# Hybrid mLSTM/pooling block: branch and output projections written out per quarter, with the pooling branch first

## The chip, the cores and the metric

One core of one Trainium2 chip. The metric is the time of one execution in microseconds, as the device measures it, of the whole kernel with the inputs in HBM. The kernel is in 32-bit floats throughout.

## The reference, cut to what matters

The layer projects 2048 latent tokens (and 256 context tokens) of width 1024 into q, k, v, gates and the inputs of a pooling branch, scans them with a two-way mLSTM, and then does this, which is all that the change touches:

```
hn  = h * rsqrt(mean(h*h per head) + eps) * head_norm_w      # h: sum of both scan directions
y_m = (hn * sigmoid(o) * silu(z_m)) @ branch_m_w             # 1024 x 1024
mixed = (box means of p - p) per group @ pool_w[group]       # 4 groups of 128
y_p = (mixed * pool_scale * silu(z_p)) @ branch_p_w          # 512 x 1024
m   = sigmoid(g_m) * y_m + sigmoid(g_p) * y_p
x   = x + gate * (m @ out_w)                                 # 1024 x 1024
out = rmsnorm(x, final_norm_w)
```

## The kernel before

Every engine's program is written out by hand, and semaphores order them. Four earlier stages (norm, two input projections, the scan with the rest of the input projection beside it) are not changed, but for two weight tiles named below. The fifth stage computes the lines above, from 2001 us to the end. It reads what the earlier stages stored in HBM: `hsum_d` (h), `u_d` (the gate of the hidden branch), `mix_d`, `zp_d` (pooling branch), `gm_d`, `gp_d` (merge gates).

The stage takes the tokens in four **quarters** of 512. Features lie on the 128 partitions. A **unit** is one block of 128 output features of one product: 8 units "m" (hidden branch, 8 feature blocks deep), 8 units "p" (pooling branch, 4 deep) and 8 units "o" (output projection, 8 deep), 24 in a quarter. Each product of 32-bit numbers is made of three matmuls of high and low parts (L1779: `wh*bh`, `wh*bl`, `wl*bh`), so that a unit m or o is 24 matmuls of 128x512, and a unit p is 12.

- Weights: SyncE loads a tile into `wraw` (2 buffers, L1625), ScalarE copies its high part to `wh` (L1823), VectorE makes the low part `wl` (L1934; 3 buffers each). A p tile is 128x512, the others are 128x1024.
- Before the units of a quarter the **hidden** inputs are made: square sums on ScalarE (L1831), norms on VectorE (L1947), 8 transposes on TensorE (`turn_hidden`, L1730), gating into `yt` (VectorE, L1958), high part `y_h` (ScalarE, L1845), low part `y_l` (GpSimd, L2064). The **pooled** inputs of a group: `mix_h` (ScalarE, L1850), `mix_l` (GpSimd, L2069), three matmuls (`group`, L1741), `ypt` (VectorE, L1968), `yp_h` (L1855), `yp_l` (GpSimd, L2073).
- `merge`: units m and p alternate. For each feature block VectorE gates both results out of PSUM (`merged_m` L2003, `merged_p` L2013), adds them (L2016), and ScalarE and VectorE split the sum into `m_h`, `m_l`.
- `out_proj`: units o. ScalarE scales a result (`of`, L1861), TensorE turns it back (`turn_output`, L1787), VectorE adds it to `xo` (L1977). In between stands the work for the next quarter: the tables NORM, GATE, SPLIT, GROUP say beside which unit.
- The final norm (`out_square` L1867, `out_stats`, `out_norm` L1988) and the store follow in the next quarter's merge.

The first quarter's preparation and merge are written out, then a hardware loop of three rounds runs `out_proj` of a quarter and `merge` of the next (`quarters`); the last `out_proj` is written out. Every queue is in order, also SyncE's, where a load that waits holds up all behind it.

Of the kernel before, what the change touches and what calls it, by code (L numbers as in the profile page):

```python
# [11 lines left out]
P = 128  # L12
D = 1024
# [11 lines left out]
PG = 4  # L25
# [21 lines left out]
def hybrid_block(nc, x, c, ctx, c_ctx, norm_w, ada_w, ada_b, in_w, gate_b, head_norm_w, pool_w,  # L47
# [29 lines left out]
    with ExitStack() as top:  # L77
# [793 lines left out]
        with ExitStack() as ph:  # L871
# [9 lines left out]
            W_BEFORE = 2 + HEADS * NU  # L881

# [84 lines left out]
            load_at = [0 if p == 1 else split_at[2 * p - 1] + 1 if p else None for p in range(NT // 2)]  # L967

# [250 lines left out]
            def _(act):  # L1219
# [60 lines left out]
                for t in range(NSLOT):  # L1280
# [7 lines left out]
                    for p in range(1, NT // 2):  # L1288
                        if load_at[p] == t:
                            pair(p)  # L1290
                    if 0 <= l + 1 < NHALF:
                        copy_scores(l + 1)
                    for m in ending(t):
                        evacuate(m)
                    for u in range(2, NT):
                        if split_at[u] == t:
                            split_hi(u)
                    if 0 <= l + 1 < NL:
                        weights_hi(l + 1)
# [7 lines left out]
            def _(dve):  # L1307
# [95 lines left out]
                for t in range(NSLOT):  # L1403
# [19 lines left out]
                    for u in range(2, NT):  # L1423
                        if split_at[u] == t:
                            split_lo(u)
                    if 0 <= l + 1 < NL:
                        weights_lo(l + 1)
# [104 lines left out]
        weights.close()  # L1532

        with ExitStack() as ph:
# [4 lines left out]
            WS = 3  # L1542
            wraw = sb("wraw5", [P, 2, KT, P])
            wh = sb("wh5", [P, WS, KT, P], FP32R)
            wl = sb("wl5", [P, WS, KT, P], FP32R)
# [20 lines left out]
            mp_ = sb("merged_p", [P, TQ])  # L1566
# [7 lines left out]
            oss = sb("oss", [P, 4, QT])  # L1574

            w_loaded = [sem(f"w5_loaded{n}") for n in range(2)]
            w_hi = sem("w5_hi"); w_lo = sem("w5_lo"); unit_done = sem("unit_done")
            rows_loaded = sem("rows_loaded"); rows_ready = sem("rows_ready")
# [8 lines left out]
            g_loaded = [sem(f"g5_loaded{n}") for n in range(2)]  # L1587
            gated = sem("gated"); m_made = sem("m_made"); m_hi = sem("m_hi"); m_lo = sem("m_lo")
            of_made = sem("of_made"); o_turned = sem("o_turned"); x_loaded = sem("x5_loaded")
            x_added = sem("x_added"); o_act = sem("o_act"); o_dve = sem("o_dve"); o_ready = sem("o_ready")  # L1590
            o_stored = sem("o_stored")


            UNITS = [(m, n, kt) for n in range(KT) for m, kt in (("m", KT), ("p", PG))] + [("o", n, KT) for n in range(KT)]
            NU = len(UNITS)
# [4 lines left out]


            NORM = {1: 0, 2: 1, 3: 2, 4: 3}
# [5 lines left out]
            def quarters(eng, out_proj, merge, last):  # L1608


                with eng.Fori(0, NTQ - 1) as i:
                    out_proj(i, True)
                    merge(i + 1, True)
                out_proj(NTQ - 1, False)
                last(NTQ - 1)

            @block.sync
            def _(sp):
                sp.sem_inc(o_stored, 1)

                def tile(i, u):
                    m, n, kt = UNITS[u % NU]
                    sp.wait_ge(w_hi, i * NU + (u + 1))
                    sp.wait_ge(w_lo, i * NU + (u + 1))
                    sp.dma_start(wraw[:, u % 2, 0:kt], SRC[m][:, :, n * P:(n + 1) * P]).then_inc(w_loaded[u % 2], 16)  # L1625

                def hidden(i, q):

                    if not isinstance(i, int):
                        sp.wait_ge(h_turned, i * QT + (q + 1 - QT))  # L1630
                    sp.dma_start(hsum[:, q], hsum_d[i * QT + q]).then_inc(h_loaded[q], 16)

                def hidden_gate(i, q):

                    sp.wait_ge(y_made, i * QT + (q + 1))
                    sp.dma_start(ut[:, q % 2], u_d[:, :, bass.ds(i * TQ + q * P, P)].rearrange("j p t -> p j t"))\
                        .then_inc(u_loaded[q % 2], 16)

                def pooled(i, g):
                    sp.wait_ge(yp_made, i * PG + (g + 1))  # L1640
                    sp.dma_start(mixt[:, g % 2], mix_d[g, :, bass.ds(i * TQ, TQ)]).then_inc(mix_loaded[g % 2], 16)
                    sp.dma_start(zpt[:, g % 2], zp_d[g, :, bass.ds(i * TQ, TQ)]).then_inc(mix_loaded[g % 2], 16)

                def gates(i, n):
                    sp.wait_ge(gated, i * (2 * KT) + (2 * n + 1))
                    sp.dma_start(gmt[:, n % 2], gm_d[n, :, bass.ds(i * TQ, TQ)]).then_inc(g_loaded[n % 2], 16)
                    sp.dma_start(gpt[:, n % 2], gp_d[n, :, bass.ds(i * TQ, TQ)]).then_inc(g_loaded[n % 2], 16)

                def store(i, q):
                    sp.wait_ge(o_ready, i * QT + (q + 1))  # L1650
                    sp.dma_start(out[bass.ds(i * TQ + q * P, P), :], xo[:, q, :]).then_inc(o_stored, 16)

                def residual_x(i, q):
                    sp.dma_start(xo[:, q, :], x[bass.ds(i * TQ + q * P, P), :]).then_inc(x_loaded, 16)

                def merge(i, after):
                    for n in range(KT):
                        tile(i, 2 * n + 3)
                        tile(i, 2 * n + 4)
                        if n + 2 < KT:  # L1660
                            gates(i, n + 2)
                        if n > KT - QT:
# [452 lines left out]
```

## Time and profile before

| | us |
|---|---|
| median of 3 runs (lowest, highest) | 2601.05 (2599.51, 2602.22) |
| the profiled execution's own time | 2600.4 |
| its span, first to last instruction | 2598.4 |
| TensorE busy (share of the span) | 2421.3 (93%) |
| VectorE, ScalarE, GpSimd busy | 1208.2, 785.4, 314.1 |
| granted TensorE clock, mean | 0.969 of full |

The span is 2.0 us below the time of the same execution, and that time is 0.65 us below the median. A share of busy time is a mean over stages; the fifth stage is the last 597 us of the span. "Issue" in the rows is idle time for which the profile shows no releaser.

### The profile page before, as it was taken

How to read it: one execution, taken by the hardware profiler on the slowest of the kernel's cores; microseconds unless marked ns; L12 is line 12 of the kernel's file. 1: busy time of each engine (PE TensorE's matmuls, PEld its weight loads, DVE VectorE, ACT ScalarE, POOL GpSimd, SP SyncE). 2: the span in 40 equal slices, each digit the busy share in tenths (PEclk: the TensorE clock that was granted, in tenths of full speed). 3: DMA queues.
4: the chain of work that ended last, by engine and by line, in shares of the span. 5: the costliest groups of instructions: out<-in, count | busy, mean ns of one | idle time of the engine just before them, and what ended most of it. 6: DMA issues, size and time to landing. Idle time of an engine off the chain costs nothing. (4 is left out here: it accounts for less than half of the span.)

```text
span 2598.4 us, 35271 instructions
## 1 busy us (share of the span) xinstructions
PE 2421.3 (93%) x12267; PEld 2018.6 (78%) x12267; DVE 1208.2 (46%) x2352; ACT 785.4 (30%) x1609; POOL 314.1 (12%) x323
## 2 busy tenths in 40 slices
PE   6897999999999998999999989999998598989897
PEld 4766888888888877888888877888887487777776
DVE  2612212212222224566666646777674555555553
ACT  2521111111111112343333323434432433343432
POOL 0011000000000001121112111321120202030300
PEclk8998999999999999999999999999999699999998
DMA  7457544534434457877787889876775574646653
GB/s 228 129 63 225 134 98 117 131 98 117 131 97 117 123 117 186 227 224 225 221 248 209 212 259 216 245 231 199 214 219 174 173 228 127 212 150 191 184 177 106
DMA packets 472916, 453.42 MB, mean 175 GB/s; under 512 B 24268, under 2 KB 414052, under 8 KB 471228
## 3 DMA queue, kind: packets, MB, share of 16 engines
q1 hardware_dynamic: 433132, 387.74, 51.2%
q10 hardware_dynamic: 32240, 32.51, 8.0%
q0 software_dynamic: 7392, 31.15, 3.1%
q8 instruction: 95, 1.56, 0.2%
q14 instruction: 57, 0.47, 0.1%
HBM read 311.25 MB, written 140.05 MB: 174 GB/s over the span
## 5 line engine op out<-in xcount | busy, mean ns | idle before, releaser
L1190 PE MATMUL bank<-xlate,wh 128*128 128x512 f32 x2048 | 673.1, 402 | 12.8 <-DVE v_t L1310 4.9
L1190 PEld LDWEIGHTS bank<-xlate,wh 128*128 128x128 f32 x2048 | 374.7, 190 | 84.1 <-DMA xlate<-xe_d 6.1
L1190 PE MATMUL bank<-xlate,wl 128*128 128x512 f32 x1024 | 411.0, 401 | 0.0
L625 PE MATMUL bank<-xearly,wh 128*128 128x512 f32 (+1 forms) x1280 | 368.5, 373 | 0.2 <-issue 0.2
L625 PE MATMUL bank<-xlate,wh 128*128 128x512 f32 x1024 | 321.3, 395 | 0.0
L625 PEld LDWEIGHTS bank<-xearly,wh 128*128 128x128 f32 x1280 | 229.3, 189 | 40.2 <-issue 0.7
L625 PE MATMUL bank<-xearly,wl 128*128 128x512 f32 (+1 forms) x640 | 237.4, 371 | 0.0
L625 PEld LDWEIGHTS bank<-xlate,wh 128*128 128x128 f32 x1024 | 190.7, 189 | 39.3
L1190 PEld LDWEIGHTS bank<-xlate,wl 128*128 128x128 f32 x1024 | 194.3, 190 | 34.4
L625 PE MATMUL bank<-xlate,wl 128*128 128x512 f32 x512 | 201.2, 393 | 0.0
L831 DVE SCALAR_TENSOR_TENSOR qks<-bank,qks 128x512 fp32r<-128x512 f32 (+1 forms) x72 | 47.5, 661 | 304.1 <-ACT qks L701 304.1
L1934 DVE TENSOR_TENSOR wl<-wraw,wh 128x1024 fp32r<-128x1024 f32 x96 | 110.8, 1154 | 122.6 <-ACT wh L1823 122.5
L1333 DVE SCALAR_TENSOR_TENSOR state<-state,cols,bank 128x516 f32<-128x516 f32 x128 | 95.7, 748 | 120.3 <-PE bank L1151 120.3
L625 PEld LDWEIGHTS bank<-xearly,wl 128*128 128x128 f32 x640 | 120.6, 188 | 21.2
L1823 ACT ACTIVATE wh<-wraw 128x1024 fp32r<-128x1024 f32 x96 | 87.3, 909 | 148.9 <-DMA wraw<-in_branch_p_w_dram 84.5
L1164 PE MATMUL bank<-state_h,q_t 128*128 128x258 f32 x512 | 114.7, 286 | 10.1 <-DVE den L1389 10.1
L1151 PE MATMUL bank<-v_t,ek_h 128*128 128x258 f32 x576 | 112.0, 286 | 7.4 <-DVE ek_l L1315 7.4
L625 PEld LDWEIGHTS bank<-xlate,wl 128*128 128x128 f32 x512 | 96.4, 188 | 21.9
L1779 PE MATMUL bank<-m_h,wh 128*128 128x512 f32 x256 | 105.8, 413 | 6.2 <-DVE wl L1934 5.6
L1304 ACT ACTIVATE ysb<-bank 128x258 f32<-128x258 f32 x128 | 49.5, 386 | 198.2 <-PE bank L1151 197.7
L1779 PE MATMUL bank<-y_h,wh 128*128 128x512 f32 x256 | 101.3, 396 | 8.2 <-POOL y_l L2064 6.6
L1338 DVE TENSOR_TENSOR wl<-wraw,wh 128x1024 fp32r<-128x1024 f32 x62 | 79.2, 1278 | 59.0 <-ACT wh L1238 59.0
(226 smaller groups left out, 4103.5 us busy)
## 6 DMA issues: line engine op xcount, KB each, us to landing
v_t<-vk_d SPq DMA_DIRECT2D x144, 384.0 KB, 4.3
qk_d<-qks SPq DMA_DIRECT2D x64, 512.0 KB, 2.7
q_t<-qk_d SPq DMA_DIRECT2D x128, 256.0 KB, 5.5
wraw<-in_in_w_dram ACTq DMA_DIRECT2D x31, 1024.0 KB, 11.9
wraw<-in_in_w_dram SPq DMA_DIRECT2D x32, 512.0 KB, 9.0
vk_d<-vs SPq DMA_DIRECT2D x64, 256.0 KB, 2.7
k_t<-qk_d SPq DMA_DIRECT2D x64, 256.0 KB, 6.6
wraw<-in_branch_m_w_dram SPq DMA_DIRECT2D x32, 512.0 KB, 4.0
```

Of the source, the lines that this page charges most:

```text
L625: mm = pe.matmul(bank[m % 4][:, 0:w], a[:, u % 2, k, :], xn(b, k, t0, w), start=(k == 0 and n == 0), stop=(k == KT - 1 and n == 2))
L831: dve.scalar_tensor_tensor(out=qks[:, a % 2, 0:cw, 1, :], in0=bank[m % 4][:, 0:w].rearrange("p (c t) -> p c t", t=P), scalar=HD ** -0.5 if ...
L1151: mm = pe.matmul(ubank[:, b, 0:VW], e_[:, L, b * P:(b + 1) * P], v_t[:, V, va, :], start=(n == 0), stop=(n == 2))
L1164: pe.matmul(XBANK[:, 0:VW], q_t[:, l % QS, b, qa, :], c_[:, L, b, :], start=(b == 0 and n == 0), stop=(b == HB - 1 and n == 2))
L1190: mm = pe.matmul(bank[m % 2][:, :], a[:, u % 2, k, :], xlate[part][:, k, tq * TQ:(tq + 1) * TQ], start=(k == 0 and n == 0), stop=(k == KT ...
L1304: act.activation(ysb[:, :], YBANK[:, 0:VW], ACT.Copy).then_inc(y_read, 1)
L1333: dve.scalar_tensor_tensor(out=state[:, ch], in0=state[:, ch], scalar=col(d, NC + latent_chunk(l), 4, h), in1=upair[:, :, 0:VW], op0=ALU.m ...
L1338: dve.tensor_tensor(wl[:, u % 2], wpair[:, :, u % 2 * P:(u % 2 + 1) * P], f32(wh[:, u % 2]), ALU.subtract).then_inc(w_lo, 1)
L1779: mm = pe.matmul(dst[:, :], a[:, u % WS, k, :], b[:, k, :], start=(k == 0 and r == 0), stop=(k == kt - 1 and r == 2))
L1823: act.activation(wh[:, u % WS, 0:kt], wraw[:, u % 2, 0:kt], ACT.Copy).then_inc(w_hi, 1)
L1934: dve.tensor_tensor(wl[:, u % WS, 0:kt], wraw[:, u % 2, 0:kt], f32(wh[:, u % WS, 0:kt]), ALU.subtract).then_inc(w_lo, 1)
```

## The change

The loop is gone: all four quarters are written out, and a quarter has three phases. Pooled phase: the 8 units p. The gated results are held in `mp_`, which now lies over the buffer `hsum` (freed as its tokens are turned). Hidden phase: the 8 units m, each result merged with the held one. Output phase: the 8 units o.

- Weights of the pooling branch come as 4 tiles 128x1024, each for two units, so that a quarter has 20 tiles and not 24. The buffers are those of the scan's stage; the first two tiles are loaded and split there, in its last slots.
- SyncE loads tile T+4 in step T, after tile T+2 has been split. The other loads of a step stand behind it.
- First quarter: all four groups come first, and `pw` is waited for alone (before: together with `hw_row`). Its hidden inputs are normed and turned after units p1, p3, p5, p7.
- Later quarters: groups before units o1, o2, o4, o5, each split a step earlier; token tile 0 turned before o5, tile 1 before o7, tiles 2 and 3 after the units p3 and p5 of the new quarter.
- The final norm's squares are taken in two parts: 896 columns once 7 of 8 blocks are added, then 128; the statistics are one instruction longer. In the last quarter the first part stands ahead of the last `output`.

```diff
+            def gate_pooled(i, n):                       # VectorE, into the held results
+                dve.wait_ge(unit_done, i * NU + n + 1)
+                dve.wait_ge(gp_loaded[n % 2], 16 * ((i * KT + n) // 2 + 1))
+                if n % 2 == 0:
+                    dve.wait_ge(h_turned, i * QT + n // 2 + 1)
-            NORM = {1: 0, 2: 1, 3: 2, 4: 3}
-            GATE = {3: 0, 4: 1, 5: 2, 6: 3}
-            SPLIT = {1: 0, 3: 1, 4: 2, 6: 3}
-            GROUP = {2: 0, 4: 1, 5: 2, 7: 3}
+            SPLIT = {0: 0, 1: 1, 3: 2, 4: 3}
+            GROUP = {1: 0, 2: 1, 4: 2, 5: 3}
+            NORM = {1: 0, 2: 1, 3: 2, 4: 3}
+            TURN_O = {5: 0, 7: 1}
+            TURN_P = {1: 2, 2: 3}
+            # pooled unit n, TensorE
+                if n < 2: pe.wait_ge(yp_made, (i + 1) * PG - 1 + n)
+                else:     pe.wait_ge(p_gated, i * KT + n - 1)
+            # ScalarE, pooled phase of a later quarter
+                if i and t == 0: output(i - 1, KT - 1)
+                split_hi(T + 2)
+                if t == 0:
+                    hidden_hi(i, 1)
+                    for q in range(QT): out_square(i - 1, 0, q)
+                if t == 1:
+                    for q in range(QT): out_square(i - 1, 1, q)
+                if t == 2: out_root(i - 1)
+                if t in TURN_P: hidden_hi(i, TURN_P[t])
+            # SyncE, output phase, step n
+                tile(T + 4)
+                if n < QT: hidden(i + 1, n)
+                if n in (2, 3): pooled(i + 1, n)
```

GpSimd during one output phase of a loop round. First before (`mix_l` is what a group waits for, `y_l` the low part of 128 turned tokens):

```order
L2064 TENSOR_TENSOR y_l<-yt,y_h 128x8x128
L2068 REGISTER_ALU
L2069 TENSOR_TENSOR mix_l<-mixt,mix_h 128x512
L2064 TENSOR_TENSOR y_l<-yt,y_h 128x8x128
L2068 REGISTER_ALU
L2069 TENSOR_TENSOR mix_l<-mixt,mix_h 128x512
L2073 TENSOR_TENSOR yp_l<-ypt,yp_h 128x512
L2064 TENSOR_TENSOR y_l<-yt,y_h 128x8x128
```

Now the same work of one quarter:

```order
L2153 TENSOR_TENSOR mix_l<-mixt,mix_h 128x512 x2
L2157 TENSOR_TENSOR yp_l<-ypt,yp_h 128x512 x2
L2153 TENSOR_TENSOR mix_l<-mixt,mix_h 128x512 x2
L2157 TENSOR_TENSOR yp_l<-ypt,yp_h 128x512 x2
L2148 TENSOR_TENSOR y_l<-yt,y_h 128x8x128 x4
```

No `mix_l` stands behind a `y_l` of its quarter any more.

VectorE at the turn from an output phase to the pooled phase. Before, from the last round's second merge step (`merged_p` is the gating of a unit p):

```order
L1934 TENSOR_TENSOR wl<-wraw,wh 128x1024
L2003 SCALAR_TENSOR_TENSOR merged_m<-gmt,bank 128x512
L1933 REGISTER_ALU
L1934 TENSOR_TENSOR wl<-wraw,wh 128x512
L2013 SCALAR_TENSOR_TENSOR merged_p<-gpt,bank 128x512
```

Now, in the last quarter (`hsum<-gpt,bank` is the same gating, into the held results; `yt` is the gating of turned tokens):

```order
L1996 TENSOR_TENSOR wl_c<-wraw,wh_c 128x1024
L2065 TENSOR_TENSOR xo<-bank,xo 128x4x128
L2018 TENSOR_TENSOR yt<-bank,ut 128x512 x2
L2038 SCALAR_TENSOR_TENSOR hsum<-gpt,bank 128x512 x2
L1996 TENSOR_TENSOR wl<-wraw,wh 128x1024
L2038 SCALAR_TENSOR_TENSOR hsum<-gpt,bank 128x512 x2
L2018 TENSOR_TENSOR yt<-bank,ut 128x512 x2
L1996 TENSOR_TENSOR wl<-wraw,wh 128x1024
L2071 TENSOR_TENSOR oss<-oss 128x4
L2073 TENSOR_SCALAR oss<-oss 128x4
L2075 RECIPROCAL oss<-oss 128x4
L2038 SCALAR_TENSOR_TENSOR hsum<-gpt,bank 128x512 x2
```

The gating of units p2, p4 and p6 now stands behind a weight split, and that behind ScalarE's work.

ScalarE at the end of the program (`of` is `output`, `junk_o` a square sum). Before:

```order
L1861 ACTIVATE of<-bank,mgate 128x512 x4
L1867 ACTIVATE junk_o,oss<-xo 128x1024 x4
L1871 ACTIVATE oss<-oss 128x4
```

Now:

```order
L1916 ACTIVATE of<-bank,mgate 128x512 x3
L1926 ACTIVATE junk_o,oss<-xo 128x896 x4
L1916 ACTIVATE of<-bank,mgate 128x512
L1926 ACTIVATE junk_o,oss<-xo 128x128 x4
L1931 ACTIVATE oss<-oss 128x4
```

Four square sums moved ahead of the last `output`.

## Rows read from the trace of the kernel before

**Rows 1.** Stretches of the fifth stage: start:end, length, busy of each engine, clock, DMA.
```profile
2001.50:2054.40 52.90, 12.96 (x44) 9.09 (x45) 29.57 (x47) 22.07 (x54) 19.46 (x12) 0.57 0.65 199
2054.40:2059.90 5.50, 5.50 (x13) 4.33 (x14) 0.83 (x1) 0.00 (x0) 0.00 (x0) 0.50 0.32 95
2054.40:2582.90 528.50, 490.89 (x2176) 401.60 (x2176) 275.29 (x379) 184.58 (x328) 62.81 (x36) 0.97 0.56 170
2582.90:2598.40 15.50, 0.66 (x4) 0.42 (x4) 6.59 (x8) 5.04 (x10) 0.00 (x0) 0.59 0.34 135
```

**Rows 2.** TensorE's waits, 2054 to 2583: us in total, times, longest.
```profile
PE bank L1741 <- issue: 24.7, 11, 3.7
PE bank L1779 <- DVE wl L1934: 12.3, 7, 2.6
PE bank L1779 <- POOL y_l L2064: 6.6, 1, 6.6
```

**Rows 3.** TensorE in order of time: start, length; without and after a long pause.
```profile
2114.30 0.39 PE L1779 MATMUL bank<-y_h,wh 128*128 128x512 f32 x1
...
2115.21 0.39 PE L1779 MATMUL bank<-y_l,wh 128*128 128x512 f32 x1
...
2152.46 0.63 PE L1779 MATMUL bank<-m_l,wh 128*128 128x512 f32 x1
2152.89 0.63 PE L1779 MATMUL bank<-m_h,wl 128*128 128x512 f32 x1
```

**Rows 4.** TensorE, pauses (us idle before, in brackets).
```profile
2151.38 0.47 PE L1741 MATMUL bank<-mix_h,pw_h 128*128 128x512 f32 x1 [3.16 <-issue]
...
2246.29 0.49 PE L1779 MATMUL bank<-y_h,wh 128*128 128x512 f32 x1 [1.59 <-DVE wl L1934]
...
2253.83 0.49 PE L1779 MATMUL bank<-yp_h,wh 128*128 128x512 f32 x1 [1.79 <-DVE wl L1934]
```

**Rows 5.** GpSimd in order of time, before the pause that ends at 2151.38.
```profile
2147.71 2.35 POOL L2064 TENSOR_TENSOR y_l<-yt,y_h 128x1024 fp32r<-128x1024 f32 x1 [7.13 <-ACT y_h L1845]
2150.02 1.26 POOL L2069 TENSOR_TENSOR mix_l<-mixt,mix_h 128x512 fp32r<-128x512 f32 x1
```

**Rows 6.** Groups, 2054 to 2583: busy us, mean ns of one, idle before.
```profile
L1934 DVE TENSOR_TENSOR wl<-wraw,wh 128x1024 fp32r<-128x1024 f32 x63 | 80.8, 1283 | 69.9 <-ACT wh L1823 69.9
L1823 ACT ACTIVATE wh<-wraw 128x1024 fp32r<-128x1024 f32 x62 | 65.0, 1049 | 34.4 <-PE bank L1779 18.9 <-DMA wraw<-in_out_w_dram 15.3
L2064 POOL TENSOR_TENSOR y_l<-yt,y_h 128x1024 fp32r<-128x1024 f32 x13 | 30.8, 2370 | 63.8 <-ACT y_h L1845 63.8
...
L2013 DVE SCALAR_TENSOR_TENSOR merged_p<-gpt,bank 128x512 f32<-128x512 f32 x32 | 21.9, 683 | 15.4 <-PE bank L1779 15.4
...
L1958 DVE TENSOR_TENSOR yt<-bank,ut 128x512 f32<-128x512 f32 x24 | 15.3, 676 | 0.0
```

**Rows 7.** Loads, 2060 to 2583: count, KB each, median us from issue to landing.
```profile
hsum<-hsum_d SPq DMA_DIRECT2D x12, 512.0 KB, 7.6
...
mixt<-mix_d SPq DMA_DIRECT2D x12, 256.0 KB, 5.5
```

**Rows 8.** The 32 loads of `gpt`, 256 KB each.
```profile
DMA to landing us min/median/max: 3.6/4.0/6.9
```

**Rows 9.** ScalarE's first instruction of the fifth stage.
```profile
2014.61 0.63 ACT L1910 ACTIVATE pw_h<-pw 128x512 fp32r<-128x512 f32 x1 [12.72 <-DMA hw_row<-in_head_norm_w_dram]
```

**Rows 10.** VectorE: two of a tile's four norms, beside GpSimd and without it.
```profile
2022.29 1.90 DVE L1947 SCALAR_TENSOR_TENSOR hsum<-hsum,hss,hw_row 128x256 f32<-128x256 f32 x2
...
2134.41 0.88 DVE L1947 SCALAR_TENSOR_TENSOR hsum<-hsum,hss,hw_row 128x256 f32<-128x256 f32 x2
```

**Rows 11.** The end of the chain that ended last: start, us, what.
```profile
2582.45 0.69 ACT of L1861
2583.15 0.05 issue
2583.19 0.67 PE bank L1787 x4
...
2584.61 1.16 ACT junk_o L1867 x2
...
2585.85 1.16 ACT junk_o L1867 x2
```

More of the change, by code:

```diff
@@ L1653, in residual_x @@
[L1653 to L1662, printed above, removed]
-                            q = n - (KT - QT + 1)
-                            if after:
-                                sp.wait_ge(o_stored, (i - 1) * (16 * QT) + (16 * (q + 1) + 1))
-                            residual_x(i, q)
-                        if after and n >= KT - QT:
-                            store(i - 1, n - (KT - QT))
@@ new lines, in hidden_unit, with ready @@
+                def hidden_unit(i, n):
+                    weights_ready(i * NT5 + M0 + n)
+                    if n >= 2:
+                        pe.wait_ge(m_gated, i * KT + n - 1)
+                    elif i:
+                        pe.wait_ge(of_made, (i - 1) * KT + KT - 1 + n)
+                    def ready(k):
+                        if n == 0 and k == 0:
+                            pe.wait_ge(y_hi, (i + 1) * QT)
+                            pe.wait_ge(y_lo, (i + 1) * QT)
+                    products(bank[n % 2], weight(i * NT5 + M0 + n), (y_h, y_l), 0, KT, ready)
@@ L1788, in turn_output @@
                     mm.then_inc(o_turned, 1)
-                def merge(i, after):
-                    for u in range(2 * KT):
-                        unit(i, u)
-                        if after and u == 0:
+                pe.wait_ge(pw_lo, 1)
+                for g in range(PG):
+                    group(0, g)
+                for i in range(NTQ):
+                    for n in range(KT):
+                        pooled_unit(i, n)
+                        if i and n == 0:
                             turn_output(i - 1, KT - 1)
-                def out_proj(i, ahead):
+                        if i == 0 and n % 2 == 1:
+                            turn_hidden(0, n // 2)
+                        elif i and n % 2 == 1 and n // 2 in TURN_P:
+                            turn_hidden(i, TURN_P[n // 2])
@@ L1980, in out_stats @@
                 def out_stats(i):
[L1981 to L1985 removed]
+                    a = i * (2 * QT + 1)
+                    dve.wait_ge(o_act, a + 2 * QT)
@@ L2047, in _ @@
-                for q in range(QT + 1):
-                    if q < QT:
-                        norms(0, q)
-                    if q > 0:
-                        branch(0, q - 1)
-                        gate_hidden(0, q - 1)
-                    if q in (1, 2):
-                        split_lo(0, q - 1)
-                dve.wait_ge(rows_loaded, 48)
-                merge(0, False)
-                quarters(dve, out_proj, merge, last)
+                branch(0, 0)
+                branch(0, 1)
@@ L2059, in _ @@
+                i = NTQ - 1
+                residual(i, KT - 2)
+                residual(i, KT - 1)
+                out_stats(i)
+                for q in range(QT):
+                    out_norm(i, q)
             @block.gpsimd
```

673 lines of the change are left out of this document (377 added, 296 removed).

## The prediction

> **What bounds the kernel now.** I read the waits of TensorE first, then cut the last stage into stretches. From 2054.4 to 2582.9, 528.5 us, TensorE is busy for 490.9 us [rows 1], and its waits there are 24.7 us ahead of groups and 12.3 us on the weights' low part (plus 0.6 us in a wait not shown) [rows 2]: 37.6 us in all, the whole idle time. VectorE is busy for 275 us of the stretch, so no helper engine is full; what waits is order. Ahead of the stretch lie 52.9 us with 13.0 us of TensorE, behind it 15.5 us with 0.7 us [rows 1]. So the fifth stage takes 596.9 us, and for 92 us of that TensorE idles (39.9, 37.6 and 14.8).
>
> A pause has a second price. Matmuls of 128x512 start every 0.227 us at the full clock (0.91 us for four) and every 0.43 us after a long pause [rows 3]: the two levels of 2.4 and 1.2 GHz. After the 3.16 us pause 10 matmuls run slowly, 1.7 us more; after 1.79 us too, after 1.59 us not [rows 4]. In order of time I count nine such runs of 7 to 10 matmuls behind nine pauses of 1.79 us or more, together 14.7 us, and one of 12 at 2054.4 (2.4 us; the clock is 0.50 of full for 5.5 us [rows 1]). The full-clock work of the stretch is therefore 528.5 - 37.6 - 17.1 = 473.8 us.
>
> **The head, 2001.5 to 2054.4.** Three things move. First, ScalarE begins only when `hw_row` has landed, at 2014.6, for the sake of `pw` [rows 9]; `pw` is a fifth of the 1.3 MB issued until then and now goes first, so I put the first group at 2014 instead of 2020.9. Second, the four groups run without hidden tiles between them; but `ypt` has one buffer, and each later group waits for the split of the one before and for a load that waits for a gating. With 5.5 us for a `mixt` load [rows 7] I follow them to 2028.5, when unit p0 begins; its last quarter waits to 2033 because ScalarE takes tile 0's square sums and root ahead of the last `yp_h`. Third, the pooled units then run between the norms. Per pair of units (5.5 us at the full clock) VectorE has a weight split of 1.28, two gatings of 0.68, two of 0.68 for `yt` [rows 6], and four norms: two of them take 1.90 us beside GpSimd and 0.88 without it [rows 10], so up to 3.8, with half a microsecond for the root. That is 8.3 at the worst and 6.2 at the best; I take 7.3 from the walk, since about half of the norms lie beside a `y_l` of 2.37 us. Four pairs from 2033 less the part of p0 already done give 2061; then the last tile needs its weight split, gatings, `y_h` (1.05, as a split of that size) and `y_l` (2.4): the hidden phase begins at 2067. The second weight tile of the branch adds a split of 1.28 us to VectorE's last slot of the scan: 1.1 us more. Head: 66.9 us instead of 52.9, but with 8 pooled units in it, 8 x 12 x 0.227 = 21.8 us. Net gain 7.8. Bounds: 60 us (loads land at once, norms without GpSimd) to 76 us (loads as long as `hsum`'s 7.6 [rows 7]).
>
> The Trainium skill (SBUF — State Buffer, "Who interferes with whom") says that a VectorE operation with two SBUF inputs and a GpSimd operation exclude each other for a whole instruction. The stretched norms agree with it. By that rule each norm or split that meets a `y_l` of 2.37 us could wait for all of it; over four pairs the head would then be about 4 us longer than by the rows.
>
> **The output phases (three with a next quarter).** Now a group waits mostly because GpSimd makes a `y_l` of 2.35 us and only then `mix_l` [rows 5]. The pauses are about 3.2 to 3.7 us twice a quarter, 0.3 to 1.3 otherwise, 24.7 us in all [rows 2]. With the new order no `mix_l` is behind a `y_l`, and the turned tiles were normed steps earlier, so these waits go. What is late next are the loads: SyncE's step n now begins after the split that follows the end of unit o(n-1), about 2.5 us into unit o(n), where a split done one unit earlier released it. `mixt` for group 2 is issued at about 17.0 us of the phase, lands 5.5 to 6 later, takes 0.6 on ScalarE (as the 128x512 copy of [rows 9]) and 1.3 on GpSimd [rows 5], and is ready at 25.1 when TensorE wants it at 24.5; group 3 likewise 1 us late. Sum 1.7 us; if `hsum` takes its full 7.6 us [rows 7], ScalarE is later too and the phase loses 5.5, with one such half-clock stretch. I take 2.5 per phase, nearer the short case, as the loads of a step are now 1 to 1.5 MB and were 2 MB. 3 x 2.5 = 7.5 us; bounds 0 and 17.
>
> **The pooled phases (three behind an output phase).** The weight waits of 12.3 us [rows 2] came from p tiles loaded in short steps; a tile now serves 5.5 us of units and is loaded four tiles ahead, 22 us against a split of 1.05 + 1.28 and a load: no wait. But gating is behind other work. ScalarE in step 0 does `output`, a split, `y_h`, and four square sums at a pitch of 1.24 us for 1024 columns [rows 11], about 1.13 for 896. `y_h` waits for VectorE's `yt` until 5.5; the squares end at 11.1; the next split at 12.2 and its low part at 13.4; only then is unit p2 gated, at 14.1, and TensorE wanted that bank for p4 at 12.5. Pause 1.65 us. The same way p6 waits 0.85 us (the statistics are in front), and the hidden phase begins on `y_l` with no pause to speak of. Sum 2.6 us. The first pause lies between the 1.59 that kept the clock and the 1.79 that lost it [rows 4], so half of a half-clock stretch, 0.8 us, is added: 3.4 per phase, 3 x 3.4 = 10.2 us. Bounds 1 and 24, the latter being the second rival.
>
> **The hidden phases** hold 5.44 us of matmuls per unit against 3.4 us of VectorE (a split of 1.28 and three steps of 128x512 at 0.68 or 0.69 [rows 6]), 1.7 of ScalarE (1.05 and 0.63): no loss. The output phase's first unit asks for the last `m_l` 2.9 us after the last unit m, and uses it at 4.8: none. The written-out code costs nothing that I can see: the first merge is written out already and runs at 0.227 [rows 3]. The Trainium skill (Runtime: NRT & Kernel Launch, "Instruction fetch mechanics") says that a taken branch out of the fetched window stalls; no pause at a loop's edge is left unexplained here, so I count no gain.
>
> **The tail.** The last `of` (0.69) starts at once after the last unit, then turning 0.67, addition 0.7, four square sums at 1.24 [rows 11]. Now ScalarE's queue has the four sums of 896 columns ahead of the last `of`, and they wait for block 6, 1.3 us after the unit. They end at 5.8; `of`, turning and addition end at 8.0. A copy of 512 columns takes 0.63 [rows 9] and of 1024 takes 1.05 [rows 6], 0.82 ns a column, so a sum of 128 columns has a pitch of 1.24 - 0.73 = 0.5 (and one of 896 of 1.13); four end at 10.0, against 7.1 before. With the extra instruction (0.2): +3.1 us. Bounds 0 and 4.
>
> **Sum.** Before: 52.9 + 528.5 + 15.5 = 596.9. After: head 66.9; then 473.8 - 21.8 = 452.0 of work, 2.4 of slow clock after the 6 us pause at the head's end, 7.5 and 10.2: 472.1; tail 18.6. Together 557.6, which is 39.3 less. The profiled execution took 2600.4 us, so 2561.1; the median of the runs is 0.65 above it: 2562.
>
> **The rivals.**
> 1. *The queues are as good as they look in the first merge*: no pause in the output phases and only the short one in the pooled phases, as the losses I add (17.7 us) come from a walk with uncertain landings. For it: 22 us of lead for weights, lighter traffic. Against: the square sums' place is certain. 4 us of loss instead of 17.7 and 2 off the head: 2546.
> 2. *The merge gates' loads pace the pooled phases.* `gpt` has two buffers; a load starts after a gating, and two units later its data is needed. Before, two units meant 16 us, now 5.5. For it: landing took up to 6.9 us [rows 8], and a 512 KB weight tile is now issued ahead of it. Then a pair takes 6.9 + 0.7 + 0.1 = 7.7 instead of 5.5: 6.7 us in three pairs, in four quarters 27, less the 10.2 that it replaces: 2579; with 1.7 at half clock behind half of the twelve pauses up to 2589. Against: the median is 4.0 us, and 4.8 fits under 5.5.
> 3. *Slower: the late loads of the output phase hold up ScalarE's in-order queue.* Square sums wait for `hsum`, then the split, `of` and `mix_h` behind them, so each of the four groups and the turns wait as two do now. Price: a pause of 3.7 and 1.7 for the clock at each of four groups, 21 us a phase, 63 in three, less the 7.5 that it replaces: 2618. It decides from 16 us a phase up (39.3 / 3 + 2.5), that is with landings of 10 us or more after issue. The longest median is 7.6 [rows 7], and there is less traffic per step; so it is unlikely.
> 4. *The change doesn't shorten anything*: the four quarters are still bound by the same chain, the pauses only change places, 2601. The rows speak against it, as the pauses have named causes that the order removes.
>
> **How the numbers follow.** My forecast, 2549 to 2574: 0.60. Rival 1, below 2549: 0.15. Rival 2, 2574 to 2595: 0.19. Rival 4: 0.02. Rival 3: 0.04. The head's bounds are -7 and +9, the phases' -17 and +24, the tail's -3 and +1; not all fall on one side, so the range of 8 in 10 is 2543 to 2583. A measurement of this kernel tells about 0.2% (5.2 us) from no change. Faster by more: 0.94; within: 0.02; slower: 0.04.
>
> **What would show it.** In the new profile: the groups' 24.7 us of waits fall below 6; the weights' 12.3 us to nearly 0; the first group starts near 2014 and the hidden phase near 2067; a pause of 1 to 2 us ahead of unit p4 in three quarters, released by the gating; after the last unit four square sums before `of`, and a tail of 18.6 us. The prediction is wrong if pauses ahead of pooled units repeat at every pair with `gpt` as the releaser of the gating (rival 2), if groups wait for `mix_l` behind a load (rival 3), or if the first quarter's pooled units take over 9 us a pair.

## The result and the profile after

| | before | after |
|---|---|---|
| median of four runs, us | 2600.28 (2597.1 to 2602.22) | 2510.23 (2509.72 to 2513.99) |
| ratio | | 0.9658 [0.9641, 0.9675] |
| profiled execution; its span | 2600.4; 2598.4 | 2509.72; 2507.9 |
| scan begins / ends, us of the span | 970.3 / 2001.5 | 946.6 / 1957.7 |
| fifth stage, scan's end to the span's | 596.9 | 550.2 |

The forecast was 2562 us in a range of 2543 to 2583. The change gained 90 us, not 39, and the time lies below the range. (In later sets of runs the kernel before took 2592 to 2597 us; against that the gain is 82 to 87 us.) The spans of the two profiled executions differ by 90.5 us, and these fall into two parts: 46.7 us in the fifth stage (forecast 39.3), and 43.8 us in front of it (forecast 0), where the code differs only in two weight tiles that are loaded and split in the scan's last slots.

The stretches of the fifth stage after, which answer to [rows 1] (head, first to last unit, tail; start:end, length, busy us of TensorE, its weight loads, VectorE, ScalarE and GpSimd with their instructions, clock, DMA share, GB/s):

```profile
1957.70:2026.20 68.50, 34.21 (x141) 25.39 (x140) 38.78 (x58) 24.34 (x56) 19.68 (x12) 0.77 0.63 200
2026.20:2489.10 462.90, 452.47 (x2080) 372.19 (x2080) 260.75 (x353) 180.23 (x331) 61.14 (x36) 1.00 0.59 185
2489.10:2507.90 18.80, 1.12 (x4) 0.72 (x4) 6.77 (x9) 6.56 (x18) 0.00 (x0) 0.61 0.28 112
```

TensorE's waits after, from 2026 us on, which answer to [rows 2] (us in total, times, longest):

```profile
PE bank L1782 <- DVE hsum L2038: 7.1, 6, 1.3
PE bank L1782 <- POOL y_l L2148: 6.3, 1, 6.3
PE bank L1840 <- ACT of L1916: 5.8, 1, 5.8
PE bank L1774 <- issue: 2.8, 3, 1.5
```

The groups' 24.7 us are 2.8, the weights' 12.3 us are none, and the pooled units of the later quarters wait six times for a gating (`hsum` is here the tile that holds the gated products). The 6.3 us end the head, the 5.8 us are the tail's.

The earlier stages: TensorE's longest waits before its last stage, first of before, then of after.

```profile
PE bank L216 <- DMA aw<-in_ada_w_dram: 12.9, 5, 3.2
PE bank L596 <- ACT ymaj L698: 11.0, 1, 11.0
PE bank L1164 <- DVE den L1389: 10.1, 4, 3.9
PE bank L1151 <- DVE ek_l L1315: 7.4, 4, 2.3
```
```profile
PE bank L216 <- DMA aw<-in_ada_w_dram: 10.2, 8, 3.5
...
PE bank L596 <- ACT ymaj L698: 5.4, 1, 5.4
PE bank L1172 <- DVE den L1407: 5.2, 4, 1.8
...
PE bank L1159 <- DVE ek_l L1333: 0.6, 1, 0.6
```

The same waits stand in both, shorter after. ScalarE's instructions are the same in both kernels up to the scan, so they tell where the 43.8 us lie: 5.0 us by its 41st instruction (76.4 us before, 71.4 after), 18.3 between the 81st and the 161st (112.8 to 384.4 before, 107.9 to 361.2 after), 0.5 from there to the scan's begin, and 20.0 in the scan. The first 5 us are chance: the other kernels whose scan ends late reach that instruction at 70.7 to 72.8 us, those whose scan ends early at 70.9 to 75.3.

The DMA queues differ too. For 117 to 900 us (queue; packets, MB, share of 16 engines' time), before and after:

```profile
q1 hardware_dynamic: 99941, 84.88, 45.7%
```
```profile
q1 hardware_dynamic: 103843, 87.12, 37.4%
```

For 4% more packets the transfer engines are busy for a fifth less: 16 x 783 us x 0.457 / 99,941 is 57 ns for a packet before, and 45 ns after. A 512 KB weight tile of the input projection landed after 9.0 us before and 7.7 after. In the scan itself queue q1 takes 50 ns for a packet in both, and it is the queue of ScalarE's loads, q10, that differs; its row for the scan, before and after:

```profile
q10 hardware_dynamic: 32240, 32.51, 20.2%
```
```profile
q10 hardware_dynamic: 33296, 33.56, 12.7%
```

That is 103 ns and 62 ns for a packet. A packet's time is not the time that a stage loses, though: the 1024 KB tiles of this queue land after 11.9 us before and 12.6 after, and from ScalarE's 161st to its 281st instruction (384 to 845 us before) both kernels take the same 460 to 461 us, with slow packets and with fast ones.

### The profile page after: what moved, and what is told of

Read it like the earlier page. It is cut to its first block and busy times, and to the rows that moved or that the text cites. A ratio compares the mean times of both kernels' runs of the same rounds, so it can differ in the third digit from the quotient of the medians.

```text
span 2507.9 us, 34424 instructions
## 1 busy us (share of the span) xinstructions
PE 2395.1 (96%) x12267; PEld 2002.5 (80%) x12267; DVE 1204.9 (48%) x2340; ACT 787.8 (31%) x1625; POOL 315.7 (13%) x323
## 5 line engine op out<-in xcount | busy, mean ns | idle before, releaser
L625 PEld LDWEIGHTS bank<-xearly,wl 128*128 128x128 f32 x640 | 120.1, 188 | 21.3
L1356 DVE TENSOR_TENSOR wl<-wraw,wh 128x1024 fp32r<-128x1024 f32 x62 | 77.2, 1245 | 57.9 <-ACT wh L1246 57.9
L1172 PEld LDWEIGHTS bank<-state_h,q_t 128*128 128x128 f32 x512 | 88.0, 190 | 12.2 <-issue 3.7
L1996 DVE TENSOR_TENSOR wl<-wraw,wh 128x1024 fp32r<-128x1024 f32 x52 | 71.4, 1373 | 54.6 <-ACT wh L1873 54.6
L1159 PEld LDWEIGHTS bank<-v_t,ek_h 128*128 128x128 f32 x576 | 91.1, 191 | 2.6 <-issue 1.3
## 6 DMA issues: line engine op xcount, KB each, us to landing
wraw<-in_in_w_dram ACTq DMA_DIRECT2D x31, 1024.0 KB, 12.6
```

Of the source, the lines that this page charges most:

```text
L625: mm = pe.matmul(bank[m % 4][:, 0:w], a[:, u % 2, k, :], xn(b, k, t0, w), start=(k == 0 and n == 0), stop=(k == KT - 1 and n == 2))
L1159: mm = pe.matmul(ubank[:, b, 0:VW], e_[:, L, b * P:(b + 1) * P], v_t[:, V, va, :], start=(n == 0), stop=(n == 2))
L1172: pe.matmul(XBANK[:, 0:VW], q_t[:, l % QS, b, qa, :], c_[:, L, b, :], start=(b == 0 and n == 0), stop=(b == HB - 1 and n == 2))
L1356: dve.tensor_tensor(wl[:, u % 2], wpair[:, :, u % 2 * P:(u % 2 + 1) * P], f32(wh[:, u % 2]), ALU.subtract).then_inc(w_lo, 1)
L1996: dve.tensor_tensor(l, wraw[:, T % 2], f32(h), ALU.subtract).then_inc(w_lo, 1)
```

## The experiments

"Scan" is its begin and end. "Blocks" are the packets of q8, of 16 KB each (95 for 1.56 MB): of the two queues that the page calls "instruction" it is the one that grows with TensorE's program. "q1" is that queue's share in 117 to 900 us, "q10" the time of one of its packets, which all lie in the scan. The kernel before was run again beside each set (medians 2592 to 2597 us); the ratios are to that, but for after's. Everything behind the ratio is of one profiled execution each. The medians and fifth stages of h2, k1, k2, k3 and m1 hold the unused work at the end, so that only their earlier stages are compared; m1 was run once.

| run | median, us | ratio, 95% | blocks | q1 | q10, ns | scan | fifth stage |
|---|---|---|---|---|---|---|---|
| before | 2600.28 | | 95 | 45.7% | 103 | 970.3 to 2001.5 | 596.9 |
| after | 2510.23 | 0.9658 | 104 | 37.4% | 62 | 946.6 to 1957.7 | 550.2 |
| e1_unrolled | 2549.63 | 0.9812 [0.9795, 0.9828] | 103 | 37.1% | 61 | 947.1 to 1955.7 | 593.5 |
| e2_pad_before | 2596.29 | 1.0001 [0.9991, 1.0010] | 95 | 46.4% | 104 | 969.5 to 1996.9 | 596.8 |
| e3_pad_after | 2511.31 | 0.9668 [0.9651, 0.9685] | 103 | 36.7% | 61 | 950.7 to 1956.4 | 552.3 |
| f1_sync_only | 2591.38 | 0.9991 [0.9977, 1.0005] | 95 | 45.7% | 103 | 966.9 to 2001.0 | 591.6 |
| f2_all_but_sync | 2552.08 | 0.9829 [0.9808, 0.9850] | 103 | 37.3% | 61 | 946.1 to 1954.6 | 597.2 |
| h1_tensor_only | 2551.75 | 0.9831 [0.9803, 0.9858] | 103 | 37.2% | 62 | 945.1 to 1952.2 | 597.4 |
| h3_three_engines | 2591.70 | 0.9994 [0.9978, 1.0009] | 95 | 45.8% | 103 | 965.8 to 2000.6 | 592.2 |
| k2_vector_length | 2656.18 | 1.0238 [1.0221, 1.0255] | 95 | 45.7% | 103 | 967.7 to 1995.2 | 658.3 |
| k1_half_length | 2621.98 | 1.0108 [1.0085, 1.0131] | 99 | 46.1% | 94 | 960.3 to 1977.1 | 641.6 |
| h2_long_program | 2652.12 | 1.0228 [1.0201, 1.0255] | 103 | 39.0% | 65 | 945.0 to 1948.6 | 700.3 |
| m1_longer_still | 2803.08 | | 112 | 47.6% | 96 | 954.2 to 1980.4 | 820.6 |
| k3_after_longer | 2638.47 | 1.0164 [1.0143, 1.0184] | 112 | 47.6% | 94 | 950.7 to 1975.0 | 662.8 |
| e4_pool_order | 2599.68 | 1.0017 [1.0002, 1.0032] | 95 | 45.8% | 104 | 966.7 to 2003.3 | 596.7 |
| g2_act_order | 2571.92 | 0.9910 [0.9890, 0.9930] | 95 | 45.8% | 103 | 969.0 to 1997.2 | 575.6 |
| g1_after_gates_tail | 2510.80 | 0.9676 [0.9657, 0.9695] | 103 | 37.1% | 61 | 947.2 to 1954.4 | 553.6 |
| j1_reordered | 2509.20 | 0.9677 [0.9652, 0.9702] | 103 | 37.1% | 61 | 945.5 to 1952.6 | 551.2 |
| j2_earlier_turns | 2511.15 | 0.9678 [0.9662, 0.9695] | 103 | 37.6% | 61 | 942.7 to 1948.3 | 558.4 |
| j3_last_low_half | 2501.01 | 0.9638 [0.9614, 0.9662] | 103 | 36.9% | 60 | 948.1 to 1955.0 | 543.7 |

### Where the 44 us of the earlier stages come from

**e1_unrolled**: the kernel before, its fifth-stage loop written out.
```diff
-                with eng.Fori(0, NTQ - 1) as i:
+                for i in range(NTQ - 1):
```


> The kernel before with only the hardware loop of the fifth stage written out (same order on every engine, same buffers). Two things are measured: where the scan ends (before 2001.5 us, changed kernel 1957.7 us) and the length of the fifth stage (before 596.9 us). Theory A (the earlier stages got 43.7 us shorter because the program has no loop at its end, or is longer): the scan ends at 1958 +- 6, total near 2556. Theory B (it is where the program's buffers lie in HBM, which any rebuild may shift): the scan's end moves by any amount or not at all, and the fifth stage stays near 597. Theory C (the changed kernel's edits in the scan stage do it): the scan ends at 2001 +- 4, total near 2600.

The scan's end moves by 46 us, the fifth stage by 3. So the gain in front of the fifth stage is no work of the new order, nor of the two tiles in the scan's last slots; writing out alone brings it.

**e2_pad_before, e3_pad_after**: unused rows in the first scratch tensor of either kernel.
```diff
-    gates_d = scratch("gates_d", (NGATE, TOK))
+    gates_d = scratch("gates_d", (NGATE + 112, TOK))[0:NGATE]
```


> The kernel before with 1.03 MB of unused rows added to its first scratch tensor in HBM; no instruction differs but for addresses. Theory A and C: nothing moves, scan end 2001 +- 4, total 2600 +- 5. Theory B (placement in HBM): the scan's end moves by more than 8 us either way, with the landing times of the weight loads of the second stage.

> The changed kernel with the same 1.03 MB of unused rows in its first scratch tensor. Theory A and C: nothing moves, scan end 1958 +- 4, total 2510 +- 5. Theory B: the scan's end moves by more than 8 us, up to back where it was before (2001), total 2515 to 2555.

Neither moves: shifting the scratch tensors by this amount does nothing.

**f1_sync_only, f2_all_but_sync**: the loop written out on some engines (here f1's condition).
```diff
+                if eng is nc.sync:
+                    for i in range(NTQ - 1): ...
+                else:
                     with eng.Fori(0, NTQ - 1) as i: ...
```


> The kernel before with the fifth stage's hardware loop written out on SyncE alone; the loop stays on the other four engines. Theory A1 (what slows the transfers of the four earlier stages is that SyncE's program holds the loop, with its transfers at addresses taken from a register): the scan ends at about 1957 us of the span instead of 2001, and the kernel takes about 2552 us. Theory A2 (it is the loop on the other engines, or the length of their programs): the scan ends near 1998 to 2003 us and the kernel takes about 2597 us. In both the fifth stage stays at 594 to 598 us.

> The counterpart of the run before this one: the loop written out on TensorE, ScalarE, VectorE and GpSimd, and kept on SyncE. Theory A1: about 2597 us, scan end near 2000. Theory A2: about 2552 us, scan end near 1957. If both of the two runs gain in part, each engine's share is read from the two scan ends.

SyncE, whose transfers take their addresses from the loop's register, is not it: A1 is out.

**h1_tensor_only, h3_three_engines**: the same with TensorE alone, and with ScalarE, VectorE and GpSimd.

> The kernel before with the fifth stage's loop written out on TensorE alone (the engine whose program grows most); loop kept on the other four. Theory P (TensorE's program is what matters, as its loop or as its length): scan end about 1956 us instead of 2001, kernel about 2552 us. Theory Q (it is the program of ScalarE, VectorE or GpSimd): scan end near 1998 to 2003, about 2593 us.

> The counterpart: the loop written out on ScalarE, VectorE and GpSimd, kept on TensorE and SyncE. Theory P: nothing, about 2593 us, scan end near 2000. Theory Q: about 2552 us, scan end near 1956. A share in both of the single runs would say that it goes by total length.

All of it sits in TensorE's program. That leaves its loop or its length:

**h2_long_program**: every loop kept, unused work behind TensorE's last instruction.
```diff
                 quarters(pe, out_proj, merge, lambda i: turn_output(i, KT - 1))
+                for _ in range(1100):
+                    pe.transpose(bank[0][:, 0:P], ident[:, :], ident[:, :])
```


> The kernel before, every loop kept, with 1100 unused transposes of the unit matrix at the very end of TensorE's program, where they run after the last real one (they lengthen the end by about 1100 x 0.06 to 0.13 us, 50 to 130 us, less what lies beside the 15 us of tail; only the earlier stages are compared). Theory L (the length of the program, and so where things lie in memory or how instructions are fetched, is what matters): scan end near 1956 us, and the queue q1 busy 37% of the window 117 to 900 us as in the unrolled kernel. Theory M (it is the loop itself): scan end near 2000, q1 at 46%.

The scan ends at 1948.6, 52 us sooner than in h3 beside it, for instructions that run only after everything else. It is the length, not the loop. Its queue q1 of 117 to 900 us, and that of h3:

```profile
q1 hardware_dynamic: 103983, 87.31, 39.0%
```
```profile
q1 hardware_dynamic: 100096, 84.95, 45.8%
```

**k1_half_length** (550 transposes), **k2_vector_length** (1104 unused one-column instructions on VectorE), **k3_after_longer** (1100 transposes behind the changed kernel), **m1_longer_still** (2200 behind the kernel before):

> The kernel before with 550 unused transposes (1100 instructions with their weight loads) behind TensorE's program instead of 1100 transposes. Only the earlier stages are compared. Theory S (a step: where the program or what is laid out behind it comes to lie in memory flips the transfers from one speed to the other): scan end either near 2000 or near 1950 us, q1 busy either 46% or 37 to 39% of the window 117 to 900. Theory G (gradual with length): scan end near 1975.

> The kernel before with 1104 unused one-column instructions behind VectorE's program, loops kept, TensorE's program as it was. If the length of any engine's program will do: scan end near 1950 us. If it takes TensorE's: near 2000 us. The end of the kernel is longer by some 70 to 150 us of these instructions and isn't compared.

> The changed kernel with 1100 unused transposes behind TensorE's program. If the fast transfers go with lengths beyond some point: scan end stays at 1950 to 1958 us. If they alternate with where things come to lie: it may fall back to about 2000 us. I take the first for likelier, 3 to 1.

> The kernel before, loops kept, with 2200 unused transposes behind TensorE's program, so that about as many blocks of instructions are fetched as for the changed kernel made longer (112). Only the earlier stages are compared. Theory R (the speed goes with the place that the length of TensorE's program gives to something, and comes and goes with it): scan end near 1975 us, q1 busy 46 to 48% of the window 117 to 900. Theory T (longer than the old program is enough; the changed kernel made longer lost its 20 us for another reason): near 1949 us, q1 37 to 39%.

VectorE's length does nothing clear of the spread. TensorE's does, in both directions: 95 blocks end the scan at 1995 to 2003, 99 at 1977, 103 and 104 at 1948 to 1958, 112 at 1975 and 1980. k1, k2, k3 and j2 were run side by side (1977, 1995, 1975, 1948), so that the differences are not between sets. The changed kernel, made longer, gives back 17 us, against my 3 to 1. The shares bear out that the transfers are slower again. The queue q1 of m1, at 58 ns a packet:

```profile
q1 hardware_dynamic: 102208, 86.00, 47.6%
```

It is neither a clean step nor a steady gain. In the scan the time goes with q10's packets: 103 or 104 ns with 1027 to 1037 us, 94 to 96 ns with 1017 to 1026, 60 to 65 ns with 1004 to 1011. In front of it q1's packets tell less: k1, m1 and k3 have them as slow as before, and their scans still begin at 960, 954 and 951 us, where kernels with 95 blocks have 966 to 970 and those with 103 have 943 to 951. So the length is shown as the cause. That slower packets are what makes the stages longer is not; and what the length moves (where something lies in memory, which channels meet) no run shows. Both stay open.

### The fifth stage

**e4_pool_order**: before, GpSimd splits the mix tile ahead of the hidden tile.
```diff
-                        if n in GATE: hidden_lo(i + 1, GATE[n])
                         if n in SPLIT: pooled_lo(i + 1, SPLIT[n])
                         if n in GROUP: branch_lo(i + 1, GROUP[n])
+                        if n in GATE: hidden_lo(i + 1, GATE[n])
```


> The kernel before with one change inside its loop: GpSimd makes mix_l and yp_l ahead of y_l. If the groups' 24.7 us of waits come from y_l standing ahead of mix_l, each long pause falls from 3.2-3.7 us to about 1 us and its half-clock stretch of 1.7 us goes too: six of each, so the fifth stage is 24 to 28 us shorter, total near 2574. If they come from the loads or from ScalarE's order instead, the pauses stay and the total is within 5 us of before.

Nothing gained: the groups still wait 22.4 us, and 4.8 us come ahead of turned tiles. So `mix_l` behind `y_l` [rows 5] was not, by itself, what the groups waited for. ScalarE had the same order one step up the chain; e4, start, length, instruction, idle before it:

```profile
2157.27 1.06 ACT L1845 ACTIVATE y_h<-yt 128x1024 fp32r<-128x1024 f32 x1 [3.30 <-DVE yt L1958]
...
2158.24 0.61 ACT L1850 ACTIVATE mix_h<-mixt 128x512 fp32r<-128x512 f32 x1
2158.92 1.27 POOL L2069 TENSOR_TENSOR mix_l<-mixt,mix_h 128x512 fp32r<-128x512 f32 x1 [6.81 <-ACT mix_h L1850]
...
2160.29 0.77 PE L1741 MATMUL bank<-mix_h,pw_h 128*128 128x512 f32 x1 [1.91 <-issue]
```

`mix_h` stands in ScalarE's queue behind `y_h`, which waits for `yt`, and GpSimd starts the moment `mix_h` is there.

**g2_act_order**: e4, and on ScalarE `pooled_hi` ahead of `hidden_hi` in the same way.

> The kernel before, loop kept, with the next quarter's pooled split ahead of the hidden split on ScalarE and on GpSimd alike (the earlier run had it so on GpSimd alone). Theory G1 (TensorE's waits at the mixing groups come from ScalarE's y_h standing ahead of mix_h, as the earlier run's trace suggests): pauses before the groups of steps 4, 5 and 7 all fall under 0.6 us, and the fifth stage is 8 to 15 us shorter: 2582 to 2590 us. Rival G2 (the step is bound by the chain turned tile, gate, split, whichever stands first, so the wait only moves to the turned tile or the first hidden unit): within 3 us of 2597.

TensorE's waits from 2048 us in g2:

```profile
PE bank L1779 <- DVE wl L1934: 13.3, 7, 2.6
PE bank L1730 <- DVE yt L1958: 10.3, 6, 2.7
...
PE bank L1741 <- issue: 0.8, 2, 0.6
```

The groups' waits go from 24.7 [rows 2] to 0.8 us; 10.3 come back ahead of turned tiles. The fifth stage is 21.3 us shorter, more than I expected: some 13 us of waits, and 8 us because, from the first unit on, 45 matmuls of 128x512 start at half clock and not 86. The two swapped orders are worth nearly half of what the rebuilt stage is. ScalarE's alone was not run.

**g1_after_gates_tail**: after, with VectorE's gatings ahead of the weight split and the last `of` first (the latter's lines).
```diff
-                for q in range(QT):
-                    out_square(i, 0, q)
                 output(i, KT - 1)
+                for q in range(QT):
+                    out_square(i, 0, q)
```


> The changed kernel with two orders altered. VectorE: in the pooled steps of quarters 2 to 4 the gates of the pooled units stand ahead of the low half of the weight split and of the norm statistics (and gate 0 ahead of the hidden gate). ScalarE: in the tail the last output copy stands ahead of the four long square sums. My reading of the trace (the pauses of 1.05 and 1.32 us before pooled units 2 and 4 come from VectorE's order, the 5.84 us in the tail from ScalarE's): the pooled pauses go (3 x 2.4 = 7.1 us) and the tail is 2.3 to 2.5 us shorter, together 9.5 us less than the changed kernel: about 2501 us. Rival (the pooled pauses are set by the bank or by the landing of the gate tiles, and the low halves of the weights now come late): the pauses stay or turn into waits on the weights, and only the tail's 2.4 us come, 2508 us.

(The units there called 2 and 4 are p4 and p6, counted from 0.) The tail is 2.4 us shorter (16.4 for 18.8), but the six pauses only shrink from 7.1 to 6.0 us, and the first hidden units now wait 6.0 us for `y_l`: nothing gained. VectorE, ready early, stands idle for the gate tile of unit p2:

```profile
2127.05 1.22 DVE L1996 TENSOR_TENSOR wl<-wraw,wh 128x1024 fp32r<-128x1024 f32 x1
2132.93 1.32 DVE L2038 SCALAR_TENSOR_TENSOR hsum<-gpt,bank 128x512 f32<-128x512 f32 x2 [4.66 <-issue]
```

SyncE issued it at 2128.8, behind a weight tile that waited for the split; a `gpt` load takes 4.4 us here.

**j1_reordered**: g1, and SyncE issues gate tiles ahead of the weight tile (the lines below) and the last mix tile a step sooner; VectorE gates the turned tile ahead of the weight split too.
```diff
+                        if i and t < M0 - 1:
+                            gate_p(i, 2 * t + 2)
+                            gate_p(i, 2 * t + 3)
                         if T + 4 < NTQ * NT5:
                             tile(T + 4)
```


> The changed kernel with five orders altered: the two of the run g1 (gates ahead of the weight split on VectorE, the last output copy ahead of the square sums), and, since the trace of g1 has gate 2 waiting on its gate tile, which SyncE issues behind a weight tile: in quarters 2 to 4 SyncE issues the next two pooled gate tiles ahead of the weight tile; VectorE gates the turned hidden tile ahead of the weight split too; and SyncE issues the last mix tile of the next quarter one step earlier. My reading (the pauses of later pooled phases were paced by the gate tiles' landing, those of the output phases by the mix tile's): the pauses before pooled units 2 and 4 fall from 1.0 + 1.3 to under 0.5 us together, no wait on y_l, the group waits under 1 us over all three output phases: 8 to 12 us less than the changed kernel: 2498 to 2502 us. Rival (the weight tile, issued later now, is late for its unit, or the pauses move to the next thing as in g1): 2507 to 2511 us.

The pauses at p4 and p6 are gone, and the groups' are 1.7 us, but the phase then ends in the chain that was hidden behind it, and the total is after's (2509.20 us):

```profile
PE bank L1786 <- POOL y_l L2154: 10.0, 3, 3.3
PE bank L1778 <- issue: 1.7, 3, 0.9
```

**j2_earlier_turns**: j1 with the turns one pair of units earlier.

> The kernel j1 with the turned hidden tiles 2 and 3 of quarters 2 to 4 one pair of pooled units earlier on TensorE, and the gate tile that goes with the last one loaded one step earlier. My reading (j1's pooled phases have no pause left, and the 3.3 us before each first hidden unit is the chain turned tile, gate, y_h, y_l behind the last pooled pair): these 3 x 3.3 us go, about 10 us less than j1: 2496 to 2500 us. Rival (the single buffer yt, which GpSimd's subtraction of 2.4 us must have read before the next gate, makes the chain as late as before, or the turned tile waits on it in the middle of the phase): 2505 to 2510 us.

The rival held. The one `yt` buffer passes the delay on, 6.2 us at the turns and 6.1 at the hidden units, 12.3 instead of j1's 10.0; and 47 matmuls of 128x512 start at half clock, not 25, another 4 us. The fifth stage is 7.2 us longer than j1's.

```profile
PE bank L1765 <- DVE yt L2022: 6.2, 3, 2.1
PE bank L1786 <- POOL y_l L2154: 6.1, 3, 2.0
```

**j3_last_low_half**: j1 with each quarter's last `y_l` on VectorE; ScalarE also makes that tile's `y_h` ahead of the final norm's root, which the expectation doesn't name.
```diff
+                def hidden_lo_last(i):
+                    dve.wait_ge(y_hi, (i + 1) * QT)
+                    s = slice((QT - 1) * P, QT * P)
+                    dve.tensor_tensor(y_l[:, :, s], yt[:, :, :], f32(y_h[:, :, s]), ALU.subtract).then_inc(y_lo, 1)
```


> The kernel j1 (the changed kernel with five orders altered) with the low half of each quarter's last turned hidden tile subtracted on VectorE (1.22 us for 128x1024 there) instead of GpSimd (2.36 to 2.40 us). My reading (each first hidden unit waits on turned tile, gate, y_h, y_l, and nothing else): the wait of 6.28 us in the first quarter falls to about 5.1, the three of 3.3 us to about 2.1: 4 to 5 us less than j1, 2504 to 2506 us. Rival (VectorE's wait for y_h delays the weight split behind it, and weights come late): 2508 us or more.

The head's wait falls from 6.29 to 5.12 us, the other three from 3.3 to 1.3 to 1.65, now for the weights' low part as the rival had it:

```profile
PE bank L1786 <- DVE wl L2000: 3.0, 2, 1.6
PE bank L1778 <- issue: 2.0, 3, 1.2
PE bank L1786 <- DVE wl_c L2000: 1.3, 1, 1.3
```

The fifth stage takes 543.7 us, 7.5 less than j1's (4 to 5 were expected) and 6.5 less than after's, and 2501.01 us is the lowest median of all. That it beats after is likely but not shown: its interval [0.9614, 0.9662] overlaps after's [0.9641, 0.9675], the two were not run side by side, and the fifth stages of kernels with the same orders differ by up to 5.8 us (f1 591.6, h1 597.4).

## Why the prediction was wrong

**The step that failed** is the sum's first line: it took the fifth stage of the new kernel and the old time of everything else, "Before: 52.9 + 528.5 + 15.5 = 596.9 ... Together 557.6, which is 39.3 less". That unchanged code keeps its time was never written as a term, so it had neither bounds nor a rival. It was worth 44 us in the profiled executions, 5 of them chance. h1, h2, k1, k3 and m1 show what stands in its place: the length of TensorE's program moves the end of the scan by up to 52 us, and the transfer engines' time for a packet changes with it; how the one leads to the other is open. With 44 us less, the forecast would have been 2518. That the total lies below even rival 1's 2546 bears out nothing in that rival.

On writing out, the prediction said that it costs nothing and counted no gain, with the Trainium skill (Runtime: NRT & Kernel Launch, "Instruction fetch mechanics") on stalls at a taken branch beside it. Inside the stage that holds: it takes 592 to 597 us with TensorE's loop (f1, h3, before) and 593 to 597 without (e1, f2, h1), so a stall there would have to be under some 5 us in all. The gain lay in stages that the loop is not in, and that rule doesn't bear on it.

**The head** (66.9 forecast) took 68.5 us. The first group came 14.3 us after the scan's end, not 12.5. The four pairs took 8.2 us each, not 7.3: the last three each held 0.98 us of waiting for a gating and 0.42 for a norm. The term that was too small is the norms. In [rows 10] the two stretched ones lay beside a `mix_l` of 1.27 us; beside a `y_l` the four of a tile take 3.87 us, and without GpSimd some 1.7 (0.88 for two in [rows 10]):

```profile
1998.53 3.87 DVE L2007 SCALAR_TENSOR_TENSOR hsum<-hsum,hss,hw_row 128x256 f32<-128x256 f32 x4
```
```profile
1999.31 2.40 POOL L2148 TENSOR_TENSOR y_l<-yt,y_h 128x1024 fp32r<-128x1024 f32 x1 [8.67 <-ACT y_h L1891]
```

One of the four starts with the `y_l` and ends 0.3 us after it, 2.67 us long, the others take 0.47 or 0.48. So a norm that meets a `y_l` does wait for nearly all of it, as the 4 us that the prediction left out of its sum had it.

**Output phases**: 2.8 us of pauses in three, not 7.5; the loads landed sooner (`mixt` 4.8 us after, 5.5 before, `hsum` 5.2 and 7.6 [rows 7]). The direction was right, but the cause I gave was not enough: e4 shows that GpSimd's order alone [rows 5] did not make the old waits, g2 that GpSimd's and ScalarE's together did. The new order mends both, so the direction came out all the same, by luck.

**Pooled phases**: pauses at p4 and p6 in all three, released by the gating. I had 1.65 and 0.85; they are 1.05 to 1.06 and 1.32. None brought the half clock for which 0.8 was added: 7.1 us instead of 10.2. Behind VectorE's order stood SyncE's, as g1 and j1 show: with only the first mended the unit waits for the gate tile, a mild form of rival 2. The rule behind the 0.8 doesn't hold either: I counted nine pauses of 1.79 us or more with a slow stretch, but there are ten, and the second of 1.79 us (at 2391.6) left the clock full.

**The rest**: weight waits none, as forecast. The half clock behind the 6.3 us bubble cost about 1.4 us (five starts at 0.43 and one at 0.56), not 2.4. The tail 18.8 us against 18.6, with `of` behind four square sums. From first hidden unit to last unit, 472.1 were forecast and 462.9 measured.

Rivals 2 to 4 are out as cases. In the fifth stage, where the terms belong, the measured 550.2 us lies between the forecast's 557.6 and rival 1's 542.

## What to carry to other kernels

Unchanged stages are a term of the sum with a range of their own: where an edit alters the length of TensorE's program, compare where they begin and end, and the DMA time for a packet in them, before crediting the edit. Padding behind the last instruction tests that cheaply. A wait belongs to the whole chain of queues ahead of it: swapping one engine's order gave nothing while the engine above it held the same order (e4), swapping both gave 21 us (g2). In the changed kernel, each pause removed uncovered the next (g1, j1, j2); follow the chain to the instruction that is simply slow, and move that (j3).

## What the runs showed of the hardware

- 550 to 2200 unused transposes behind TensorE's program moved the end of a stage that runs before them: 21 to 53 us sooner in the kernel before, 17 us later in the changed one. 1104 instructions behind VectorE's left it at 1995; kernels with TensorE's program unchanged lie at 1997 to 2003.
- A VectorE norm of 0.47 us that started with a GpSimd subtraction of 2.40 us took 2.67 us.
- The same pause doesn't always cost clock. Of before's two pauses of 1.79 us one led to 1.2 GHz [rows 4], the other did not. Of j1's three of 3.3 us before a hidden unit, the first and third left the clock full and the second brought seven starts at 0.43 us. The rows are j1's, just behind the first and the second (clock 1.00 and 0.62):

```profile
2147.50:2152.00 4.50, 4.42 (x20) 3.70 (x21) 4.50 (x4) 0.86 (x1) 0.00 (x0) 1.00 0.52 164
2271.60:2276.10 4.50, 4.49 (x13) 3.57 (x14) 4.47 (x4) 0.60 (x1) 0.00 (x0) 0.62 0.52 160
```
